# The last square before a norm goes ahead of the weight rounding, and the root's table is loaded one block sooner

## The reference

```python
x = x + merged @ w_out[l]                    # first block
h2 = rms_norm(x, norm2_g[l])
...
x = x + (jax.nn.silu(u_gate) * u_val) @ w_down[l]
# second block, for each of 2 layers
h = modulate(rms_norm_2(x, norm_g[l, 0]), mod[:, 0, 0], mod[:, 0, 1])
x = x + 0.5 * mod[:, 0, 2][:, None, :] * swiglu(h, ffn_w_in[l, 0], ffn_w_out[l, 0])
...
return rms_norm_2(x, final_norm_g)

def rms_norm(x, g):
    y = x * lax.rsqrt(jnp.mean(x * x, axis=-1, keepdims=True) + EPS)
    return y * g
```

## Time and profile before

| | us |
|---|---|
| median of three runs | 4113.03 |
| the three runs | 4107.44 to 4114.31 |
| the profiled execution | 4119.46 |
| its span, first to last instruction | 4117.6 |
| TensorE busy (matmuls) | 3947.1 |
| VectorE busy | 1688.8 |
| ScalarE busy | 1376.8 |
| GpSimd busy | 1353.1 |

### The profile page before, as it was taken

How to read it: one execution, slowest core, us unless ns; L and a number is a source line. 1 busy time by engine, 2 the same in 40 slices (tenths; PEclk the granted TensorE clock), 3 DMA queues, 4 the chain that set the end, 5 groups by cost and what they waited for, 6 DMA issues and landing times.

```text
span 4117.6 us, 50026 instructions
## 1 busy us (share of the span) xinstructions
PE 3947.1 (96%) x20184; PEld 3287.1 (80%) x20184; DVE 1688.8 (41%) x3103; ACT 1376.8 (33%) x1864; POOL 1353.1 (33%) x298
## 2 busy tenths in 40 slices
PE   7999999999999999999899999999999989899998
PEld 7887878887788878878667978887887777898887
DVE  4777435453687454442465521102101256542100
ACT  4665324443322232222233332223223224323222
POOL 2223332222344534452101034453445210103445
PEclk9999999999999999998888999999999889999999
DMA  3211221111355645663100022232233310002233
GB/s 124 71 63 62 95 92 62 52 62 62 133 184 208 232 153 184 207 222 103 41 21 31 1 72 99 96 133 92 92 113 123 94 50 11 32 21 82 92 113 123
DMA packets 66353, 401.83 MB, mean 98 GB/s; under 512 B 7776, under 2 KB 8288, under 8 KB 27872
## 3 DMA queue, kind: packets, MB, share of 16 engines
q1 hardware_dynamic: 44624, 314.67, 21.8%
q10 hardware_dynamic: 21520, 84.16, 6.4%
HBM read 396.70 MB, written 2.10 MB: 97 GB/s over the span
## 4 chain that ended last, share of the span: by engine, by line
issue 75%; POOL 14%; PE 10%; POOLq 0%; DVE 0%; ACT 0%; DVEq 0%; ACTq 0%
POOL w_lo L331 14%; PE g L344 3%; PE g L345 3%; PE g L346 3%; PE p L405 0%; POOLq L327 0%; DVE x L1463 0%; PE p L429 0%; POOLq L330 0%; POOLq L331 0%; ACT L421 0%; ACT n_sq L413 0%; DVE h_lo L466 0%; DVE n_t L462 0%; ACT h_hi L443 0%
## 5 line engine op out<-in xcount | busy, mean ns | idle before, releaser
L331 POOL TENSOR_TENSOR w_lo<-w_raw,w_hi 128x2048 fp32r<-128x2048 f32 x294 | 1352.9, 4602 | 2753.6 <-ACT w_hi L338 2753.5
L344 PE MATMUL g<-h_hi,w_lo 128*128 128x512 f32 x2976 | 1210.3, 407 | 23.3 <-DVE h_lo L466 12.4
L346 PE MATMUL g<-h_hi,w_hi 128*128 128x512 f32 x2976 | 1180.2, 397 | 0.0
L345 PE MATMUL g<-h_lo,w_hi 128*128 128x512 f32 x2976 | 1179.7, 396 | 0.0
L338 ACT ACTIVATE w_hi<-w_raw 128x2048 fp32r<-128x2048 f32 x294 | 562.6, 1914 | 1120.5 <-PE g L346 1114.2
L344 PEld LDWEIGHTS g<-h_hi,w_lo 128*128 128x128 f32 x2976 | 572.4, 192 | 150.4 <-issue 21.3
L346 PEld LDWEIGHTS g<-h_hi,w_hi 128*128 128x128 f32 x2976 | 571.3, 192 | 124.3
L345 PEld LDWEIGHTS g<-h_lo,w_hi 128*128 128x128 f32 x2976 | 573.0, 193 | 118.3 <-issue 4.5
L344 PE MATMUL g<-act_hi,w_lo 128*128 128x512 f32 x880 | 353.0, 401 | 0.0
L345 PE MATMUL g<-act_lo,w_hi 128*128 128x512 f32 x880 | 348.4, 396 | 0.0
L346 PE MATMUL g<-act_hi,w_hi 128*128 128x512 f32 x880 | 348.2, 396 | 0.0
(11 more groups left out here) (410 smaller groups left out, 4806.9 us busy)
## 6 DMA issues: line engine op xcount, KB each, us to landing
w_raw<-in_stream SPq DMA_DIRECT2D x294, 1024.0 KB, 4.8
ada_w<-in_ada ACTq DMA_DIRECT2D x144, 512.0 KB, 4.6
n_w<-in_w ACTq DMA_DIRECT2D x8, 1024.0 KB, 14.9
x<-in_x SPq DMA_DIRECT2D x4, 512.0 KB, 6.5
out_x<-x SPq DMA_DIRECT2D x4, 512.0 KB, 2.7
masks<-in_masks SPq DMA_DIRECT2D x1, 1344.0 KB, 12.7
cols<-in_cols SPq DMA_DIRECT2D x1, 338.0 KB, 12.6
n_pos<-in_pos ACTq DMA_DIRECT2D x1, 256.0 KB, 6.4
```

The costliest lines, as they stand in the source:

```text
L331: K.nc.gpsimd.tensor_tensor(K.w_lo[:, s], K.w_raw[:, s], K.w_hi[:, s].bitcast(F32), ALU.subtract).then_inc(K.sem("w_lo"), 1)
L344: nc.tensor.matmul(out, w_lo, h_hi, start=start, stop=False)
L345: nc.tensor.matmul(out, w_hi, h_lo, start=False, stop=False)
L346: return nc.tensor.matmul(out, w_hi, h_hi, start=False, stop=stop)
```

## The change

Three edits, all in ScalarE's program. In `next_sum` the dummy root moves from ahead of block 7's square to behind block 6's. In `act_out` the last unit's two squares come ahead of the wait for `part` and the split. In `act_ffn` the square of block 7 comes ahead of the last down unit's wait and split. No instruction is added or dropped, and no other engine's program changes.

```diff
 def next_sum(K, act, pos, m):
 
-    if m == KD - 1:
-        act.activation(K.n_warm[:, 0:1], K.col("eps"), ACT.Sqrt)
     act.wait_ge(K.sem("x_ready"), pos.next("x_ready"))
     squared(K, act, pos, m)
+    if m == KD - 2:
+        act.activation(K.n_warm[:, 0:1], K.col("eps"), ACT.Sqrt)
...
 def act_out(K, act, pos):
     for u in range(4):
-        act.wait_ge(K.sem("part"), pos.next("part", 2))
-        split_unit(K, act, pos, u % 2)
+        if u < 3:
+            act.wait_ge(K.sem("part"), pos.next("part", 2))
+            split_unit(K, act, pos, u % 2)
         next_sum(K, act, pos, 2 * u)
         next_sum(K, act, pos, 2 * u + 1)
+    act.wait_ge(K.sem("part"), pos.next("part", 2))
+    split_unit(K, act, pos, 1)
...
     for u in range(NDN):
+        if u == NDN - 1:
+            next_sum(K, act, pos, u // 2)
         act.wait_ge(K.sem("part"), pos.next("part"))
         split_unit(K, act, pos, u % 2)
         loads(NUP + u)
-        if u % 2:
+        if u % 2 and u < NDN - 1:
             next_sum(K, act, pos, u // 2)
```

## The result

The changed kernel takes 4087.97 us (median of 7 runs, 4078.28 to 4098.82) against 4110.59 for the kernel before (7 runs, 4107.44 to 4114.31), a ratio of 0.9943 with a 95% interval of 0.9926 to 0.996. That is 22.6 us, twice the forecast 11.5, and outside the range given. Its profiled execution took 4078.28, the fastest of the seven, 41.2 less than the profiled one before, which at 4119.46 was slower than all seven of its own. So the two profiles lie further apart than the medians.

A forecast was written before the change was run, and what follows sets the result against it. TensorE, busy 96% of the span, was taken as the bound, so ScalarE counts only where it idles. Gains and one loss at eight boundaries summed to 11.5 us gained, 4113.03 to 4101.5 us, range 4095 to 4109.

The forecast's parts named there:

- The chain of each boundary: Between a stage's last add to the residual and the next norm: square, sum, reduce, root; eight places, 11.5 us gained.
- A: End of the last add to the residual x ahead of a norm; later times are counted from it.
- B5: Boundary from feed-forward c of layer 0 into layer 1: 2.06 us gained.
- B8: Boundary into the final norm: root 2.93 us sooner, 2.46 if the sum is slow.
- B3: Boundary from feed-forward a of layer 0 into the mixer: 2.76 us gained.
- B6: Boundary from feed-forward a of layer 1 into the mixer: 2.76 us gained.
- B2: Boundary behind the first block's feed-forward: L1452 held longer by GpSimd's L331, 1.29 us lost.
- The 0.25 given back: At B3, B5 and B6, L466 held until after GpSimd's L331 ends: 0.25 us of each gain lost.
- Rival (b): Reciprocal L451 held by GpSimd too at the boundaries: 12.5 us lost in all, 4125.5 us; chance 0.03.
- (c): Table load comes back behind the split, ahead of the root: gain cut, 4107.5 us; chance 0.05.
- Rival (a): TensorE's lower clock behind each norm gives part of the gain back: 4105.5 us; chance 0.17.
- B4: Boundary from the mixer of layer 0 into feed-forward c: idle among TensorE's sums removed, 1.27 us gained.

The follow-up runs named there:

- The early root alone: Kernel before with only the dummy root moved behind block 6's square, split and squares in the old order: 4097.76 us, ratio 0.9952.
- the order alone: Changed kernel with the dummy root put back ahead of block 7's square, squares still ahead of the splits: 4085.68 us, ratio 0.9933.
- the two families of kernels: Kernel before plus four forms with added squares, and changed kernel plus two; added work taken off, their means differ by 12 us.

## Why the prediction was wrong

- **The chain of each boundary: right.** Square at A + 0.03, root at A + 2.37 behind the split at B5 and B8, and at A + 2.50 at B3 and B6, where the sum, partly slow, came last by 0.13; seven of the eight moves lie within 0.25 us of the forecast. A fast sum took 1.05 instead of 0.92; the split hid it.
- **What the later split collides with: right, in both places.** L466 stretched to 0.89 and 1.03, 0.55 past L331 as computed; L1452 held for 3.83 and B2 1.30 longer. The 0.25 given back was 0.14, 0.28 and 0.13, and would be 1.2 with a fast spread; what I didn't see is that L331 thereby becomes the last wait of the first matmul. Rival (b) fell: the reciprocal inside L331 took 0.18. So did (c): no load stands on the root or a split. **Rival (a) fell too**: with it the stages behind the boundaries would have grown by about half of what was gained ahead of them. At B5 2.04 was gained, the clock rose 4.42 us behind the first matmul against 4.39 before, and the stage took 371.2 both times; without the mixers the feed-forwards became shorter by 0.0 to 0.6, not longer.
- **No drain behind the table load.** The early root alone gave 1.5 us at B3 and B8, which is the 1.48 of load and dummy root. The Trainium skill's further 1.38 (ScalarE: Activation LUTs, "What ACT_TABLE_LOAD costs") doesn't show here.
- **B4: mis-sized.** 1.27 was forecast and 0.37 measured: the gap went, but the clock fell earlier among the sums.
- **The early root: right in the number, wrong in the credit.** I put the load's cover one unit earlier; the order alone covers it too.
- **The step that failed is the first one, "a change on ScalarE counts only where TensorE stands idle"**, and with it the sum over eight boundaries alone: it puts the stages between them at nothing, without a reason. They don't keep their length. The lower clock is spread through the mixers, and its share there depends on where they fall among the clock's changes. I weighed the clock only for the unit behind a norm (rival a, which would have taken gain away). That was worth 28 of the 41 us of the profiles. In the medians it is some 8 to 12 of 22.6, by the two families of kernels and by the boundaries' 10.6. That this came out as a gain, and about as large as the forecast itself, is luck as far as the prediction goes: nothing in it foresees the sign.
- **The range** took its scatter from three runs of the kernel before, 6.9 us apart. Over all runs here the kernel before lies between 4098.6 and 4127.5, and the changed one spread over 20 us in seven runs; with that the low end belonged near 4080. The lower bound of the sum was off by itself as well: slow sums everywhere and B4 at 0 leave 9 us by the prediction's own terms, not 8, since a root at A + 2.84 frees L466 from the hold.
- **Still open**: why the kernel before meets the lower clock more in most of its runs (its medians in five sets are 4107 to 4120, its mean granted clock mostly 0.960 to 0.964, against 0.963 to 0.968 for the changed one), and so on which side of the mean an edit starts.

## What to carry to other kernels

Where a wait ends on an in-order queue, the work that nobody waits for goes behind it: here the new order alone brought all of the 2.9 us of a boundary, the table load included. Ask of every instruction that is moved later what its follower will run into: L331, late by 1.4 us, cost 1.3 at one boundary and 0.13 to 0.28 at three, and became what those three wait for last. A split behind the norm, tried at B2 only, is untested there. And before a gain or loss of half a per cent is credited to an edit, shift the same kernel by a microsecond of useless work at a few places: if that moves it as much, the sum over the boundaries tells the edit's own worth. A kernel without the stage that reacts most comes closer to it (15.3 against 10.7), but still holds some of the clock's part.

## What the runs showed of the hardware

A stage of short matmuls took 523 to 548 us with the same instructions, by the share of it that ran at the lower of TensorE's two levels (PEclk 0.93 to 0.89 in its windows). Which it was went with the place of its start among the clock's changes: mixers of different kernels with the first fall at 19.73 to 19.83 us took 522.9, those at 19.57 and 19.60 took 538.6. Adding 0.5 to 1.6 us of work ahead of both mixers made the whole kernel 8 to 9 us faster. An instruction of VectorE with two SBUF inputs of 512 columns ended 0.55 us after the GpSimd instruction that it met, whether it had been stretched by 0.1 us (L466, 0.89) or by 3.9 (L1214, 4.67). A reciprocal (L451, 0.18 inside L331) and instructions whose second large input lies in PSUM (the eight that scale x in the final norm took 5.36 us together, whether the first of them ran inside L331, as in the changed kernel, or none did, as before) were not held.
